# A two-layer mixing transformer on one core: ScalarE's order in the attention, the Fourier low parts, and the first output products

## The reference, cut to what matters

```python
y_f = fourier_mix(f_l)                     # real part of a 2-D FFT, 256 channels
y_ret = retention_output(ret_l, rg_l, gn_w)  # 4 heads, both directions, chunks of 128
# attention, 8 query heads on 2 key heads, blocks of 128 queries; keys: the block, its neighbours, 256 context tokens
m = max(s_loc.max(-1), s_ctx.max(-1), sink)
denom = exp(s_loc - m).sum(-1) + exp(s_ctx - m).sum(-1) + exp(sink - m)
o = (p_loc / denom) @ v_window + (p_ctx / denom) @ v_ctx
out_lat = concatenate([y_f, y_ret, y_att], axis=-1) @ w_o
```

## Time and profile before

| what | value |
|---|---|
| median of 3 runs | 2759.57 us (2758.16 to 2765.77) |
| the profiled execution | 2770.8 us, its span 2769.0 us |
| mean granted TensorE clock | 0.985 of full speed |
| TensorE busy | 2684.2 us (97%) |
| VectorE / ScalarE / GpSimd busy | 1520.8 / 691.9 / 94.8 us |
| retention turns to attention, layer 0 | about 777 to 799.7 us |
| attention, layer 0 | 799.7 to 903.7 us |
| attention, layer 1 | 2259.2 to 2340.8 us |

### The profile page before, as it was taken

The page is one execution under the profiler, slowest core; times in us unless marked ns, Lnnn a source line. Parts: engine busy times, 40 slices in busy tenths (PEclk is TensorE's granted clock), DMA queues, the critical chain, the costliest instruction groups (busy, mean ns, idle before and its releaser), DMA issues.

```text
span 2769.0 us, 42294 instructions
## 1 busy us (share of the span) xinstructions
PE 2684.2 (97%) x15515; PEld 2300.5 (83%) x15515; DVE 1520.8 (55%) x2621; ACT 691.9 (25%) x1075; POOL 94.8 (3%) x211
## 2 busy tenths in 40 slices
PE   6999999999988999999999999999999988999998
PEld 4888888888867878888888888888887867888887
DVE  5776477544366377625773677347535465533343
ACT  4111111132256231111111311111123245422222
POOL 0000000000033000000000000000000022000000
PEclk8999999999989999999999999999999999999999
DMA  7877477412200167626762577257522200233332
GB/s 230 197 183 176 116 184 185 114 51 84 61 1 1 46 148 185 163 59 161 185 169 60 123 185 176 65 142 185 130 65 84 76 16 7 80 96 106 91 100 90
DMA packets 485790, 316.89 MB, mean 114 GB/s; under 512 B 30588, under 2 KB 483664, under 8 KB 485712
## 3 DMA queue, kind: packets, MB, share of 16 engines
q1 hardware_dynamic: 485712, 315.88, 44.7%
HBM read 313.73 MB, written 2.10 MB: 114 GB/s over the span
## 4 chain that ended last, share of the span: by engine, by line
PE 90%; DVE 4%; ACT 2%; issue 2%; POOL 1%; DMA 0%; SPq 0%; POOLq 0%; DVEq 0%; ACTq 0%
PE pg L703 79%; PE pg L770 5%; PE p L718 1%; PE pn L1006 1%; DVE mx L1808 1%; PE pg L962 1%; DVE xlo L1592 1%; ACT whi L1117 1%; DVE probT L1801 1%; DVE tnorm L1584 1%; ACT prob L1325 0%; DVE wlo L1445 0%; PE p L1023 0%; PE pg L967 0%; POOL ak_lo L633 0%
## 5 line engine op out<-in xcount | busy, mean ns | idle before, releaser
L703 PE MATMUL pg<-xhi,whi 128*128 128x512 f32 x2880 | 803.5, 347 | 5.7 <-POOL xlo L633 3.7
L703 PE MATMUL pg<-xhi,wlo 128*128 128x512 f32 x2880 | 796.5, 345 | 0.0
L703 PE MATMUL pg<-xlo,whi 128*128 128x512 f32 x2880 | 796.0, 345 | 0.0
L1117 ACT CAST whi<-raw 128x1024 fp32r<-128x1024 f32 (+1 forms) x288 | 321.8, 1118 | 1075.1 <-PE pg L703 1066.4
L1445 DVE TENSOR_TENSOR wlo<-raw,whi 128x1024 fp32r<-128x1024 f32 (+1 forms) x288 | 377.7, 1312 | 351.8 <-ACT whi L1117 349.2
L703 PEld LDWEIGHTS pg<-xhi,whi 128*128 128x128 f32 x2880 | 455.4, 188 | 74.4 <-issue 4.0
L703 PEld LDWEIGHTS pg<-xlo,whi 128*128 128x128 f32 x2880 | 456.1, 188 | 71.2
L703 PEld LDWEIGHTS pg<-xhi,wlo 128*128 128x128 f32 x2880 | 455.0, 188 | 70.3
L1529 DVE SCALAR_TENSOR_TENSOR part<-ada,cond,part 128x256 f32<-128x256 f32 x960 | 465.2, 485 | 32.7
L1655 DVE SCALAR_TENSOR_TENSOR h<-pg,gcol,h 128x512 f32 (+1 forms) x118 | 71.4, 639 | 456.8 <-PE pg L703 456.8
L703 PE MATMUL pg<-ahi,whi 128*128 128x512 f32 x1100 | 307.4, 347 | 0.0
(11 more groups left out here) (206 smaller groups left out, 1966.8 us busy)
## 6 DMA issues: line engine op xcount, KB each, us to landing
ada<-in_w_ada SPq DMA_DIRECT2D x512, 256.0 KB, 4.2
raw<-in_ffn_w_in SPq DMA_DIRECT2D x176, 512.0 KB, 3.9
raw<-in_ffn_w_out SPq DMA_DIRECT2D x64, 704.0 KB, 4.5
raw<-in_w_in SPq DMA_DIRECT2D x24, 512.0 KB, 3.9
ada_first<-in_w_ada SPq DMA_DIRECT2D x8, 1024.0 KB, 12.1
raw<-in_w_in SPq DMA_DIRECT2D x16, 256.0 KB, 3.4
raw<-in_w_o SPq DMA_DIRECT2D x16, 256.0 KB, 2.7
raw<-in_w_o SPq DMA_DIRECT2D x32, 128.0 KB, 2.9
```

The lines of the kernel that those rows point to most:

```text
L703: last = nc.tensor.matmul(pg[s][:, p0:p1], w[:, s, k], v[:, k, p0:p1], start=(k == 0 and n == 0), stop=(k == kt - 1 and n == 2))
L1117: nc.scalar.copy(whi[:, s, 0:nk], raw[:, s, 0:nk]).then_inc(s_whi[s], 1)
```

## The change

Five edits, all in the two `mix` stages. ScalarE: the sink's exponential goes behind the exponential of q, and the copy `rden_t` of a pair goes from even q = 2pr + 4 to odd q = 2pr + 5. `negm` gets eight columns. VectorE: the two Fourier low parts leave the retention turns and go to the end of attention iterations q = 4 and q = 6. TensorE: the products of `wo`'s first unit for k = 0..3 are issued in iteration len(units) + 1, behind the last value products; those of k = 4..6 in the next one, behind the last transpose of reciprocals; k = 7 stays in `wo`. No operation is added or dropped.

```diff
-        negm = sb("negm", [P, 4])
+        negm = sb("negm", [P, 8])
...                                                                    (GpSimd)
-                        nc.gpsimd.tensor_tensor(esink[:, p], negm[:, p], sink[:, hd:hd + GROUP + 1:GROUP], ALU.add
+                        nm = slice(pr % 4 * 2, pr % 4 * 2 + 2)
+                        nc.gpsimd.tensor_tensor(esink[:, p], negm[:, nm], sink[:, hd:hd + GROUP + 1:GROUP], ALU.add
...                                                                    (TensorE)
+            def first_out(i, k0, k1):
+
+                l, t = phases[i][1], tokens(i)
+                if k0 == 0:
+                    pe.wait_ge(s_w[0], pair0(i) + 1)
+                    pe.wait_ge(s_free[0], read_value(i, -1))
+                pe.wait_ge(s_y[l], y_count(l) - (0 if k1 == KD else pair_units(l) // 2))
+                for k in range(k0, k1):
+                    for n, (w, v) in enumerate(((whi, xhi), (whi, xlo), (wlo, xhi))):
+                        for p0, p1 in [(0, SEQ)] + ([(SEQ, TOK)] if t == TOK else []):
+                            last = nc.tensor.matmul(pg[0][:, p0:p1], w[:, 0, k], v[:, k, p0:p1],
+                                                    start=(k == 0 and n == 0), stop=(k == KD - 1 and n == 2))
+                if k1 == KD:
+                    last.then_inc(s_unit[0], 1)
...
                     if q >= 2 and q % 2 == 0 and q <= len(units):
                         att_values((q - 2) // 2)
+                    if q == len(units) + 1:
+                        first_out(i + 1, 0, 4)
+                    if q == len(units) + 2:
+                        first_out(i + 1, 4, KD - 1)
...
-                    pe.wait_ge(s_y[l], y_count(l))
-                    with pe.Fori(0, units // 2 - 1) as j:
+                    first_out(i, KD - 1, KD)
+                    unit(i, 1, 0, xhi, xlo, t)
+                    with pe.Fori(1, units // 2 - 1) as j:
...                                                                    (ScalarE)
-                    if q >= 2 and q % 2 == 0 and q <= len(units):
-                        pr = (q - 2) // 2
-                        p = slice(pr % 2 * 2, pr % 2 * 2 + 2)
-                        act.wait_ge(s_es, pair_count(l, pr))
-                        nc.scalar.activation(esink[:, p], esink[:, p], ACT.Exp).then_inc(s_ee, 1)
...
-                        b = slice(q % 4, q % 4 + 1)
+                        b, nm = slice(q % 4, q % 4 + 1), slice(q % 8, q % 8 + 1)
                         nc.scalar.activation(prob[:, q % 2, 0:w], pg[q % 2][:, TOK - w:TOK], ACT.Exp,
-                                             bias=negm[:, b], accum_out=den[:, b]).then_inc(s_p[l], 1)
+                                             bias=negm[:, nm], accum_out=den[:, b]).then_inc(s_p[l], 1)
+                    if q >= 2 and q % 2 == 0 and q <= len(units):
+                        pr = (q - 2) // 2
+                        p = slice(pr % 2 * 2, pr % 2 * 2 + 2)
+                        act.wait_ge(s_es, pair_count(l, pr))
+                        nc.scalar.activation(esink[:, p], esink[:, p], ACT.Exp).then_inc(s_ee, 1)
...
-                    if q >= 4 and q % 2 == 0 and q < len(units) + 3:
-                        pr = (q - 4) // 2
+                    if q >= 5 and q % 2:
+                        pr = (q - 5) // 2
                         act.wait_ge(s_rT[l], pr + 1)
                         nc.scalar.copy(rden_t[:, pr % 2], pa[pr % 2][:, P:2 * P]).then_inc(s_rt, 1)
...                                                                    (VectorE)
-                    if r in (2, 5 if nt > 4 else 4):
-                        k = 0 if r == 2 else 1
-                        y_low(l, k, ysum[k][:, 0:tq], 0, tq, k + 1)
...
-                        nc.vector.tensor_scalar(negm[:, b], mx[:, b], sink[:, hd:hd + 1], -1.0, ALU.max, ALU.mult
+                        nm = slice((q + 1) % 8, (q + 1) % 8 + 1)
+                        nc.vector.tensor_scalar(negm[:, nm], mx[:, b], sink[:, hd:hd + 1], -1.0, ALU.max, ALU.mult
                                                 ).then_inc(s_nm[l], 1)
...
+                    if q in (4, 6):
+                        k = (q - 4) // 2
+                        y_low(l, k, ysum[k][:, 0:tq], 0, tq, k + 1)
```

## The result

| | before | after |
|---|---|---|
| median | 2762.67 us (2758.16 to 2766.2, 4 runs) | 2747.72 us (2744.95 to 2749.94, 4 runs) |
| ratio, 95% interval | | 0.9946 [0.9926, 0.9967] |
| profiled execution, span | 2770.8, 2769.0 | 2749.94, 2748.1 |
| granted clock | 0.985 | 0.992 |
| second session: median, ratio | 2765.88 | 2746.35, 0.9928 [0.9912, 0.9943] |

Faster, by 15 us and by 19.5 us in two sessions, which the intervals (9 to 20 and 16 to 24 us) can't tell apart; 22.5 were forecast. The profiled executions differ by 20.9, close to what was worked out for them (2748.3 forecast, 2749.94 measured).

A forecast was written before the change was run, and what follows sets the result against it. TensorE, busy 97% of the span, was taken as the bound, leaving only its waits and low-clock stretches in the mixing stages. Terms of 6.0 + 2.1 + 5.0 + 0 + 1.9 + 0.5 + 3.5 + 3.5 = 22.5 us gave 2737 us, range 2729 to 2749.

The forecast's parts named there:

- Steady attention, layer 0: Layer 0's steady attention: earlier exponentials shrink TensorE's waits until TensorE takes over; 6.0 us gained, 2.5 to 8.4.
- The slower rival: Attention: late denominators delay VectorE's reciprocal and thus every exponential; 27 us slower, 2787 us; chance 0.03.
- Steady layer 1: Layer 1's steady attention: shorter exponential waits, less 0.5 us at each of 3 switches; 2.1 us net gain, 0 to 3.5.
- The ends: Before wo in each layer: early products cover the reciprocals' wait and avoid the low clock; 3.5 us gained per layer.
- Turns, layer 0: Layer 0's retention turns: without low parts, gap and low clock go, first scores come earlier; 5.0 us gained, least 1.8.
- Opening, layer 0: Start of layer 0's attention: 3.5 us gained without low parts, which cost 1.7 and 0.5; taken as 1.9, 0 to 3.5.
- Turns, layer 1: Layer 1's retention turns: gain ends in the first scores' wait for GpSimd; 0, or up to 1.5 us lost.
- Opening, layer 1: Start of layer 1's attention: smaller gap and less low clock, less the low part's cost; 0.5 us gained, 0 to 2.0.
- the gap goes, the clock returns: Layer 1's attention opening: 0.9 us from the gap and up to 1.5 of clock, less 0.7 for the low part.
- The sum: Whole kernel: all stage gains add to 22.5 us, giving 2748.3 us for the profiled execution and 2737 for the median.
- The chain did not take over: Rival, steady attention and opening: copy, maximum and negm or GpSimd's path bound, 3 us instead of 10.5; 2744.6 us; chance 0.20.
- The edges keep the half clock: Rival, turns and openings: other gaps keep the low clock, retention gives 1.8 us, opening nothing; 2742.7 us; chance 0.15.

The follow-up runs named there:

- after_again: The changed kernel, unchanged, run and profiled again in the second session: 2746.35 us, 0.9928 of the kernel before.
- before_again: The kernel before, unchanged, under a name of its own for another profile: 2762.63 us, 0.9994.
- sink_mixed: ylow_78 with the sink's exponential ahead again in layer 1, only in pairs where GpSimd then makes the next queries' low part: 2743.37 us, 0.9922.
- order_only: The kernel before with ScalarE's order alone (sink's exponential, reciprocal copy, eight columns of negm): 2751.05 us, 0.9958.
- first_only: The kernel before with the earlier first output products of wo alone: 2760.17 us, 0.9986.
- sink_only: The kernel before with the sink's exponential moved and eight columns of negm, reciprocal copy left at even q: 2754.07 us, 0.9968.
- after_ylow_back: The changed kernel with the Fourier low parts back in the retention turns: 2744.85 us, 0.9925.
- ylow_78: The changed kernel with layer 0's low parts at the end of q = 7 and 8, layer 1's back in the turns: 2744.04 us, 0.9926.

## Why the prediction was right, and where it was not

- **Steady attention, layer 0** (-6.0): -5.96, and -5.95 in the second pair of profiles (after_again less before_again). The reading that TensorE's wait can shrink by what the exponential gains (0.42 us) and that TensorE takes over from the chain holds: the waits for an exponential fell from 8.4 to 2.5 us. The sum was right; its two parts, which I had not priced apart, are 4.0 for the sink and 1.3 for the copy, and 0.6 for both together. The slower rival has no trace: GpSimd still waits for the reciprocal in the steady stretch of after, 26.3 us in 15 waits, so the denominators are there in time.
- **Steady layer 1** (-2.1): -2.39, with 0.3 lost per switch, as sink_mixed shows, against the 0.5 taken.
- **The ends** (-3.5 each): -3.52 and -3.62. The cover of 3.1 against 2.16 us was right, in layer 1 too. But this is the profile's size: 1.7 and 1.6 us of it were half clock. before_again and order_only have none behind layer 1's gap, so it is worth 1.97 there. By the medians first_only brings 2.9 us, not 7.
- **Turns, layer 0** (-5.0): -6.35, but -3.34 from before_again. The move does what I had said (GpSimd no longer stretched, no low clock), but most of the gain is not its own: sink_only, with the low parts still in the turns, has 17.25 there, 4.9 of the 6.35 us, because the first low part takes 0.95 us in it instead of 2.60. On top of that the move brings 1.5 us. Why, is open (above); that was not among my rivals. The expected wait for GpSimd's query low parts, and the half chance of 1.7 us of low clock behind it, did not come.
- **Opening, layer 0** (-1.9): -1.71. The two sub-terms were each larger: without low parts it gains 4.3 (3.3 against before_again), where I had booked 3.5, and they cost 2.4 to 2.6, where I had 1.7 + 0.5. (3.5 less these two is 1.3; the prediction takes 1.9 and gives no reason.) The row of the first one: 806.00 + 1.82 = 807.82 is where GpSimd's instruction ends, and 0.82 later, 808.64, ends the low part, which takes 0.95 alone. By the rule of the Trainium skill, SBUF — State Buffer, Who interferes with whom, on the port pair (an exclusive lock for the whole instruction), the low part waits for GpSimd's instruction and then takes its own time; the trace agrees within 0.13 us.
- **Turns, layer 1** (0): -0.68. The gap before the first scores grew from 2.22 to 2.69 us and took part of the gain, not all.
- **Opening, layer 1** (-0.5): +2.76, and -1.21 in the second pair. This is the step that failed: "the gap goes, the clock returns". The gap of 1.86 us did shrink by the 0.9 booked, to 1.00, and the low part cost its 0.7. But the next wait, at the switch to the second t, grew from 0.45 us (before, at 2279.03) to 2.28, and the half clock, instead of returning to full as I had booked with up to 1.5 us, grew in this profile. The timeline of after at the switch to the second t, which lies in the opening:

```profile
2254.11 0.21 DVE L1835 TENSOR_SCALAR negm<-mx,sink 128x1 f32<-128x1 f32 x1
2254.24 1.17 DVE L1683 TENSOR_TENSOR xlo<-ysum,xhi 128x512 fp32r<-128x512 f32 x1
2255.33 0.55 DVE L1819 COPY probT<-pn 128x384 f32<-128x384 f32 x1
2256.51 0.21 DVE L1835 TENSOR_SCALAR negm<-mx,sink 128x1 f32<-128x1 f32 x1
...
2257.46 0.20 ACT L1347 ACTIVATE esink<-esink 128x2 f32<-128x2 f32 x1
2257.81 0.20 POOL L676 TENSOR_TENSOR rden<-den,esink 128x2 f32<-128x2 f32 x1 [0.38 <-ACT esink L1347]
2258.08 1.26 POOL L633 TENSOR_TENSOR aq_st<-z,aq_st 64x512 fp32r<-64x512 f32 x1
2259.48 0.55 PE L978 MATMUL pg<-ak_hi,aq_st 128*128 128x256 f32 x1 [2.28 <-ACT prob L1341]
```

VectorE goes from `negm` to copy, maximum and next `negm` without a pause, and the low part of 1.17 us stands in that row; exponential, sink and GpSimd's low part follow it. That ends at 2259.34 and the scores follow at 2259.48: the bracket names an exponential that had long been done. The same wait is 2.29 us in after_again; with the low parts in the turns it is 1.64 in after_ylow_back and 1.63 in ylow_78:

```profile
2255.85 0.36 PE L978 MATMUL pg<-ak_hi,aq_st 128*128 128x256 f32 x1 [1.63 <-POOL aq_st L633]
```

So the low part costs 0.65 us here. The growth from 0.45 to 1.63 comes with ScalarE's order alone (order_only has 1.63 too): it is GpSimd's path, which I had named but not priced. The whole openings say the same of the low part, 27.40 in after_again against 26.77 in after_ylow_back with 1.7 us of half clock in each: 0.6, paid for by the 0.7 of the turns. The rest of +2.76 goes with the clock: behind the 2.28 us stood 6.6 us at 0.50, which after_again doesn't have (27.40 against 31.70, behind 2.29 us). The other such stretch (7 us at 0.55) follows the 2.69 us before the first scores. This profile loses 6.8 us to half clock in layer 1, before 5.1, before_again 3.4, after_again 1.7.

- **The sum.** 22.5 was forecast, 21.5 is the sum of the eight stages, 20.9 the spans: right for the execution that it was made against. The second pair of profiles, after_again less before_again, gives 19.8: 3.3, 0.8, 6.0 and 3.5 in layer 0, and 0.7, 1.2, 2.4 and 2.0 in layer 1. Against the medians 22.5 is 3 to 7.5 us too much. Of the 10.7 us between 2737 and 2747.72, 3.1 are the median of before, 2759.57 from three runs and 2762.67 from four. The mis-sized term is the clock: I booked it as if every execution of before lost what this one did, 15.3 us in the mixing against 8.5 in before_again. The profiled one stood 8 us above the median of 2762.67, and that was the sign to discount it. 2747.72 lies inside the range only towards its slow end, 1.3 us from it, and outside the 2731 to 2744 that I had given to the forecast alone; that 21.5 came so near to 22.5 is partly luck: the turns of layer 0 were 1.35 us better and the opening of layer 1 3.3 worse.
- **The rivals.** The chain did not take over in the steady stretch. "The edges keep the half clock" came half true, in layer 1, where after lost 6.8 us to it and after_again 1.7. By the time alone both of these rivals, with 2744.6 and 2742.7, fit better than the forecast's 2737; it is the stages that tell them apart.

## What to carry to other kernels

In a strict engine queue, an instruction with slack that stands ahead of one on the critical path costs what it waits: read when its input comes, and put it behind, unless another engine's path hangs on it (in sink_mixed putting it back ahead shortened a switch by 0.33 us). Moving work out of a stretch pays only if its new place is free of the resource that made it dear (here GpSimd's instruction beside VectorE's), so measure the move alone against the rest of the change. And split a forecast into idle time, which repeated within 0.1 us in the steady stretches of all kernels with the same order, and granted clock, which didn't; take the second at a discount, above all where the profiled execution is slower than the median.

## What the runs showed of the hardware that I had not expected

- The length of a gap does not fix the clock behind it. The same gap of 1.76 us was followed by about 11 us at 0.57 of the clock in before and by 4 us in before_again. A gap of 2.23 us before layer 1's first scores is followed by half clock in sink_mixed (2236 to 2241 at 0.69 in the mean) and by none in ylow_78.
- A low part of 0.95 us alone took 2.23 and 2.52 us beside GpSimd's instruction of 1.8. Which of the two is held up does not follow from the recorded starts: GpSimd 0.02 us ahead each time, it was the low part in before (2.60 us, GpSimd 1.80) and GpSimd in order_only (2.63 us, the low part 0.95).
- Each exponential with a row sum has a second instruction of 0.19 us behind it on ScalarE. In the pair of after above it starts at 842.51 and ScalarE's next instruction at 842.60, 0.09 us later and before its recorded end.
- Three products of 512 columns in f32 took 2.84 us, as six records: more than the gap that they were to fill.
